# Stick-breaking heads without conditioning panels: nine panels move into layer one, and the scores are computed once and masked on VectorE

## The chip, the cores and the metric

One core of a Trainium2 chip runs the whole program. The metric is the device time of one execution in microseconds (us); less is better. TensorE is called PE in the rows, VectorE DVE, ScalarE ACT, GpSimd POOL, and SyncE, which issues the weight loads, SP.

## The reference

Input is x of 256 tokens by 1024 channels. A first block and two further layers follow each other. What matters here:

```python
# first block: u = rmsnorm(h); u_ssm, q, k, v = split(u @ w_in)
#   y_ssm  = s5_branch(u_ssm)                      32 groups, a linear recurrence over the tokens
#   y_attn = stick_breaking_attention(q, k, v)     8 heads of 64
#   h += (sigmoid gates * (y_ssm @ w_up_ssm, y_attn @ w_up_attn)) @ w_out;  h += relu(norm(h) @ w_ff1)^2 @ w_ff2
z = einsum("bqhd,bkhd->bhqk", q_blk, kf) * scale
mask = key_pos[None, :] < q_pos[:, None]
log_fail = where(mask, log_sigmoid(-z), 0.0)
after = cumsum(log_fail, axis=3, reverse=True) - log_fail
w = where(mask, exp(log_sigmoid(z) + after), 0.0)
# layers 0 and 1 (depth 2):
ada = c_act @ w_ada + b_ada        # (1, 3072) a layer; c_act = silu(c)
shift, scale, gate = split(ada, 3)
u = x * (1 + scale) + shift        # ... convolutions, latent attention of 8 heads, merge, w_o
```

## The kernel before

All activations lie in SBUF with channels on the partitions. The weights (about 177 MB) stream from HBM in **panels** of at most 1 MB, in the order that `schedule()` writes out by hand. Every engine walks this one list `ORDER` from front to back and does its own part of each step, so an engine that waits holds back all later steps of its own.

A panel lands in one of four slots of `raw` (`RAW = 4`, by its index in the list). ACT rounds it to `w_hi` (L842), DVE or POOL computes the rest `w_lo` (L1122, L744; POOL for gate panels 2 to 7 and the feed-forward), and PE does 48 matmuls of 256 columns, three for each product (L1617 to L1619). `w_hi` and `w_lo` have three slots (`HL = 3`); `next_splits` works ahead by at most three split panels, and from a split panel by fewer than four places of the list, from a conditioning panel by fewer than two.

Results go to two PSUM banks in turn, `pg[g % 2]`, where `g` counts the groups of all panels. `group_start(g)` makes PE wait until group `g - 2` has been read out (`take`, L848 on ACT, L1149 on DVE).

A **conditioning panel** (`ada_panel(i)`, 24 of them, 12 a layer) isn't split: PE reads it from `raw` (L1651) and gives its slot back itself. It takes a group like the others. `ada_take(i)` reads that bank on ACT into `root[:, 1, :]`, and `ada_turn(i)` (L1732, PE) turns it into two columns of a PSUM bank. `ada_end(part)` adds the bias on DVE.

The stick-breaking attention runs together with the recurrence of the first block, in eight **turns** m = 0 to 7 (and a last one, 8). In a turn:

- PE: `stick_fails(m)` (the scores a second time into `p_c`, then three products with `ntri` and `nones`), `ada_turn(m)`, `stick_scores(m+1)` into `p_z`, `bu(2m+1)` and `bu(2m+2)` (L1756), the gate panel m, `s5_out(m-1)` (L1773), `stick_out(m-1)`, and conditioning panel m+1. `bu(r)` waits for `state(r-2)`.
- DVE: `stick_weights(m-1)`, `stick_soft(m)`, `state(2m)` and `state(2m+1)`: eight instructions each on `p_bu` or `p_s` and the table `waves`. `state(r)` waits for `bu(r)` and, from r = 4, for `s5_out((r-4)/2)`.
- ACT: Exp of the weights, the rounding of a panel, Abs, Exp and Ln of the scores, and the sigmoids of the gate.
- POOL: the tables (L793 to L797) and `w_lo` of the gate panels. Before the turns it builds the block-diagonal inputs of the recurrence (`s5_diag`, L762 to L769).

Layer one (`l == 0`) begins with the latent panels (`q_lat`, `kv_lat`, `k_rope`), their norms (`latent_sums`, `latent_norm`, where `root[:, 1, :]` is ACT's square root of `kv_lat` and DVE inverts it, L1167), then panels `a2`, `a1`, `uq`, `ukv`, the long convolution on DVE (`conv_a`, L1517), eight heads of latent attention with a panel beside each, the branches and merges, `w_o` and the layer norm.

Of the kernel before, what the change touches and what calls it, by code (L numbers as in the profile page):

```python
# [19 lines left out]
P = 128  # L20
T = 256
# [56 lines left out]
ADA_PARTS = ((0, 14), (14, 17), (17, 20), (20, 24))  # L78
# [12 lines left out]
def schedule():  # L91
# [74 lines left out]
    ada_panel(0)  # L166
    step("ada_take", 0)
    for m in range(HEADS + 1):
# [8 lines left out]
        step("ada_turn", m)  # L177
# [34 lines left out]
    step("ada_turn", 9)  # L212
    ada_panel(10)
    step("ada_take", 10)
    panel("up_attn", 0, 1, "w_up_attn", 0, 512, WT, 512, 2)
    step("ada_turn", 10)
    half("glu", 0, "w_glu", W)
    ada_panel(11)
    step("glu_mul")
    step("split", "yg")  # L220
    step("ada_take", 11)
    step("ada_turn", 11)
    half("up_ssm", 0, "w_up_ssm", D)
    ada_panel(12)
    step("split", "u1")
    step("ada_take", 12)
    for n in range(4):
        panel("out", 0, n, "w_out", 0, 256 * n, KT, 256, 1)
        if n < 2:
            step("ada_turn", 12 + n)  # L230
        if n == 0:
            ada_panel(13)
            step("ada_take", 13)
        if n == 1:
            step("ada_end", 0)
        if n:
            norm_sums(1, n - 1)
    norm_steps(1, "u2", 14)
    chunks = DFF // W
    for c in range(chunks + 1):  # L240
        if c < chunks:
            for n in range(2):
                panel("ff1", 0, 2 * c + n, "w_ff1", 0, W * c + 256 * n, KT, 256, 1)
                if (c, n) == (0, 0):
                    step("ada_turn", 16)
                    step("ada_end", 1)
# [7 lines left out]
    norm_steps(2, ("u", 0), 17)  # L254

    for l in range(LAYERS):
        panel("q_lat", l, 0, "w_in_2", 0, CQ, KT, 256, 1)
        if l == 0:
            step("ada_turn", 19)
            step("ada_end", 2)  # L260
        else:
            step("ada_turn", 23)
            step("ada_end", 3)
# [25 lines left out]
        for h in range(HEADS + 2):  # L289
# [21 lines left out]
        for n in range(4):  # L311
            panel("merge1", l, n, "w_in_2", 0, CM + D + 256 * n, KT, 256, 1)
            if n == 1:
                step("ln_a_mean", l)
            if n == 3:
                step("ln_a_var", l)
        half("branch2", l, "w_c_out_2", D)
        for n in range(4):
            panel("merge2", l, n, "w_in_2", 0, CM + 2 * D + 256 * n, KT, 256, 1)
            if n == 0:  # L320
                step("ln_a_out", l)
            if n == 1:
# [4 lines left out]
        if l == 0:  # L327
            step("modulate_columns", 1)
        for n in range(4):
            panel("w_o", l, n, "w_o_2", 0, 256 * n, KT, 256, 1)  # L330
            if n:
                step("ln_mean", l, n - 1)
        if l == 0:
            ada_panel(20)
        step("ln_mean", l, 3)
        if l == 0:
            step("ada_take", 20)
        step("ln_centre", l)
        if l == 0:
            ada_panel(21)  # L340
            step("ada_turn", 20)
# [42 lines left out]
def build(nc, t, out, marks, dry):  # L384
# [3 lines left out]
    with ctx:  # L388
# [82 lines left out]
        mask1 = sb("mask1", [P, 384])  # L471
# [61 lines left out]
        stick_z = tmp[:, 4:7, :].rearrange("p a n -> p (a n)").rearrange("p (a n) -> p a n", a=2)  # L533
        stick = [stick_z[:, 0], stick_z[:, 1], stick_w[:, 0], stick_w[:, 1]]
# [151 lines left out]
        def _(pool):  # L686
# [12 lines left out]
            pool.memset(mask1[:, :], 1.0).then_inc(*c.step())  # L699
# [11 lines left out]
            for lo, w in ((0, 256), (256, 128)):  # L711
                pool.affine_select(out=mask1[:, lo:lo + w], in_=mask1[:, lo:lo + w], compare_op=ALU.is_gt,
                                          fill=0.0, base=0, pattern=[[1, w]], channel_multiplier=-1).then_inc(*c.step())
# [99 lines left out]
        def _(act):  # L813
# [199 lines left out]
            def stick_scores(hd, _):  # L1013

                act.wait_ge(sem("z"), over("z", hd))
                if hd == 0:
                    act.preload_act_table_set("natural_log_exp_and_others")
                else:

                    act.wait_ge(sem("soft"), over("soft", hd - 1))  # L1020
                fn(stick[0], p_z[:, 0:384], ACT.Abs).then_inc(*c.step())
                fn(stick[0], stick[0], ACT.Exp, scale=-1.0).then_inc(*c.step())
                fn(stick[0], stick[0], ACT.Ln, bias=1.0).then_inc(*c.event("log1p", hd))
# [83 lines left out]
        def _(dve):  # L1107
# [228 lines left out]

            def stick_soft(hd, _):

                dve.wait_ge(sem("log1p"), over("log1p", hd))
                stt(stick[1], p_z[:, 0:384], 0.0, stick[0], ALU.max, ALU.add).then_inc(*c.step())  # L1340
                tt(stick[1], stick[1], mask1[:, :], ALU.mult).then_inc(*c.event("soft", hd))

            def stick_weights(hd, _):
# [3 lines left out]
                stt(stick[2 + hd % 2], p_c[:, 0:384], 0.0, neg1[:, :], ALU.min, ALU.add).then_inc(*c.event("logw", hd))  # L1347

            def ada_end(part, _):
# [3 lines left out]
                for l in range(LAYERS):  # L1353
                    a, b = max(2 * first, 24 * l), min(2 * end, 24 * l + 24)
                    if a < b:
                        ps = p_z[:, 384 + a:384 + b] if part == 0 else p_c[:, a:b]
# [227 lines left out]
            def ln(l, _):  # L1584
                invert(("var", l))
                before = c.last
                for j in range(4):
# [7 lines left out]
                         stick_soft=stick_soft, stick_weights=stick_weights,  # L1595
# [9 lines left out]
        def _(pe):  # L1605
# [109 lines left out]
            def ada_turn(i, _):  # L1715
# [3 lines left out]
                ps = p_z[:, 384:512] if part == 0 else p_c  # L1719
                if part == 0:  # L1720
                    pe.wait_ge(sem("soft"), over("soft", min(i, HEADS - 1)))
                elif i == ADA_PARTS[1][0]:
                    pe.wait_ge(sem("logw"), over("logw", HEADS - 1))
                elif part > 1 and i == ADA_PARTS[part][0]:
                    pe.wait_ge(sem("ada"), over("ada", part - 1))
                    if part == 3:
                        pe.wait_ge(sem("probs_t"), over("probs_t", 0, HEADS - 1))
# [48 lines left out]
            def qk(dst, hd, stop):  # L1776

# [180 lines left out]
```

## Time and profile before

| | |
|---|---|
| median of 3 runs | 1209.64 us (1209.32 to 1210.97) |
| profiled execution | 1214.46 us, span 1212.6 us |
| busy share of the span | PE 88%, weight loads 82%, DVE 62%, ACT 45%, POOL 22% |
| mean granted TensorE clock | 0.929 |
| DMA queue of the weights | 177.22 MB, 46.0% of 16 engines |

The profiled execution is 4.8 us above the median; differences are taken within it. Times in timeline rows count from the start of its span.

### The profile page before, as it was taken

The numbers are of one execution on the slowest core, as the hardware profiler recorded it, in microseconds if no ns is written. First come the engines' busy times: TensorE is split into PE (matmuls) and PEld (weight loads), VectorE is DVE, ScalarE is ACT, GpSimd is POOL, SyncE is SP. The second block draws the span as 40 slices with busy tenths as digits, with TensorE's granted clock in tenths as the row PEclk, the third lists the DMA queues.
The fourth block names the chain that finished last, engine by engine and source line by source line (L and its number), as shares of the span: only waits on it lengthen the run. The fifth ranks groups of instructions, "written<-read, shape, count | busy, mean of one in ns | idle before, by whom it ended". The sixth has DMA issues, their size and how long they took to land.

```text
span 1212.6 us, 19568 instructions
## 1 busy us (share of the span) xinstructions
PE 1068.3 (88%) x8104; PEld 994.2 (82%) x8104; DVE 757.4 (62%) x1096; ACT 539.8 (45%) x620; POOL 262.9 (22%) x131
## 2 busy tenths in 40 slices
PE   4989999779799999969877998998789787989985
PEld 3968777579699999969876898998689776989984
DVE  4938887453624322267877797654657877886653
ACT  4543544432444434355422653542564234636432
POOL 3096771000586887401000000000010000000000
PEclk8978999889899999989988998998899898999997
DMA  7532434546564656365342444653637332544601
GB/s 246 192 119 81 155 113 140 183 129 209 184 199 140 208 177 202 123 208 159 105 139 74 136 139 139 199 184 105 193 106 223 97 107 77 177 147 133 210 29 35
DMA packets 159495, 179.56 MB, mean 148 GB/s; under 512 B 5040, under 2 KB 141744, under 8 KB 159408
## 3 DMA queue, kind: packets, MB, share of 16 engines
q1 hardware_dynamic: 159024, 177.22, 46.0%
q8 instruction: 64, 1.05, 0.4%
q0 software_dynamic: 384, 1.10, 0.3%
q14 instruction: 23, 0.19, 0.0%
HBM read 177.26 MB, written 1.05 MB: 147 GB/s over the span
## 4 chain that ended last, share of the span: by engine, by line
PE 56%; DVE 23%; issue 9%; ACT 8%; POOL 3%; DMA 1%; SPq 0%; DVEq 0%; ACTq 0%; POOLq 0%
PE pg L1617 16%; PE pg L1618 16%; PE pg L1619 16%; DVE area L1517 7%; ACT w_hi L842 4%; DVE area L1131 3%; DVE w_lo L1122 3%; ACT area L820 2%; DVE area L1139 2%; PE p_s L1611 1%; PE p_s L1707 1%; PE p_y L1773 1%; DVE area L1135 1%; DVE mx L1538 1%; DMA raw<-in_w_in 1%
## 5 line engine op out<-in xcount | busy, mean ns | idle before, releaser
L1617 PE MATMUL pg<-u_hi,w_hi 128*128 128x256 f32 x1664 | 492.6, 296 | 60.2 <-DVE u_lo L1131 38.3
L1618 PE MATMUL pg<-u_lo,w_hi 128*128 128x256 f32 x1664 | 482.3, 290 | 0.0
L1619 PE MATMUL pg<-u_hi,w_lo 128*128 128x256 f32 x1664 | 481.8, 290 | 0.0
L1617 PEld LDWEIGHTS pg<-u_hi,w_hi 128*128 128x128 f32 x1664 | 331.5, 199 | 70.1 <-issue 46.4
L1618 PEld LDWEIGHTS pg<-u_lo,w_hi 128*128 128x128 f32 x1664 | 331.7, 199 | 0.9
L1619 PEld LDWEIGHTS pg<-u_hi,w_lo 128*128 128x128 f32 x1664 | 330.7, 199 | 0.0
L1122 DVE TENSOR_TENSOR w_lo<-raw,w_hi 128x2048 fp32r<-128x2048 f32 (+3 forms) x115 | 247.3, 2158 | 127.6 <-ACT w_hi L842 127.4
L842 ACT ACTIVATE w_hi<-raw 128x2048 fp32r<-128x2048 f32 (+3 forms) x153 | 274.9, 1803 | 73.7 <-issue 38.6
L744 POOL TENSOR_TENSOR w_lo<-raw,w_hi 128x2048 fp32r<-128x2048 f32 x38 | 176.0, 4648 | 188.2 <-ACT w_hi L842 188.2
L848 ACT ACTIVATE area<-pg 128x512 f32<-128x512 f32 (+1 forms) x92 | 54.2, 589 | 170.2 <-PE pg L1619 158.3
L1517 DVE SCALAR_TENSOR_TENSOR area<-area,par 128x256 f32<-128x256 f32 x240 | 97.8, 480 | 0.8
L1617 PE MATMUL pg<-vb_hi,w_hi 128*128 128x256 f32 x320 | 91.7, 287 | 5.7 <-issue 3.8
L805 POOL COPY area<-area 64x2048 f32<-64x2048 f32 x2 | 8.0, 4014 | 400.9 <-DVE area L1131 400.9
L1618 PE MATMUL pg<-vb_lo,w_hi 128*128 128x256 f32 x320 | 91.3, 285 | 0.0
L1619 PE MATMUL pg<-vb_hi,w_lo 128*128 128x256 f32 x320 | 91.2, 285 | 0.0
L1617 PE MATMUL pg<-va_hi,w_hi 128*128 128x256 f32 x288 | 84.2, 292 | 3.7 <-DVE va_lo L1131 3.1
L1618 PE MATMUL pg<-va_lo,w_hi 128*128 128x256 f32 x288 | 82.9, 288 | 0.0
L1619 PE MATMUL pg<-va_hi,w_lo 128*128 128x256 f32 x288 | 82.9, 288 | 0.0
L1131 DVE TENSOR_TENSOR area<-area 128x512 f32<-128x512 f32 (+6 forms) x78 | 49.8, 638 | 34.2 <-ACT area L848 31.0
L1617 PEld LDWEIGHTS pg<-vb_hi,w_hi 128*128 128x128 f32 x320 | 62.0, 194 | 6.5 <-issue 4.9
L1149 DVE TENSOR_TENSOR h<-pg,h 128x512 f32<-128x512 f32 x36 | 24.9, 692 | 66.3 <-PE pg L1619 65.5
L820 ACT ACTIVATE area<-area 128x384 f32<-128x384 f32 (+6 forms) x67 | 37.1, 554 | 65.4 <-DVE area L1396 51.6
(200 smaller groups left out, 1327.3 us busy)
## 6 DMA issues: line engine op xcount, KB each, us to landing
raw<-in_w_in SPq DMA_DIRECT2D x68, 1024.0 KB, 5.3
raw<-in_w_ff SPq DMA_DIRECT2D x32, 1024.0 KB, 5.6
raw<-in_w_ada SPq DMA_DIRECT2D x24, 1024.0 KB, 5.1
raw<-in_w_gate SPq DMA_DIRECT2D x8, 1024.0 KB, 7.6
raw<-in_w_o SPq DMA_DIRECT2D x8, 1024.0 KB, 5.1
raw<-in_w_out SPq DMA_DIRECT2D x4, 1024.0 KB, 6.6
raw<-in_w_b_out SPq DMA_DIRECT2D x4, 1024.0 KB, 5.0
raw<-in_w_c_out SPq DMA_DIRECT2D x4, 1024.0 KB, 5.0
```

The costliest lines, as they stand in the source:

```text
L744: pool.tensor_tensor(w_lo[:, s, 0:n], raw[:, r, 0:n], w_hi[:, s, 0:n].bitcast(F32), ALU.subtract).then_inc(sem(f"raw_free{r}"), 1)
L820: return act.activation(out_, in_, func, **kw)
L842: act.activation(dst, src, ACT.Copy).then_inc(*(c.event("w_hi", q["s"]) if i == len(parts) - 1 else c.step()))
L848: act.activation(dst, src, func, **kw).then_inc(*c.bank_free(g))
L1122: ins = dve.tensor_tensor(dst, src, hi.bitcast(F32), ALU.subtract)
L1131: return dve.tensor_tensor(out_, a, b, op)
L1139: return dve.scalar_tensor_tensor(out=out_, in0=a, scalar=s, in1=b, op0=op0, op1=op1)
L1149: dve.tensor_tensor(out_, a, b, op).then_inc(*c.bank_free(g))
L1517: ins = dve.scalar_tensor_tensor(out=acc[:, j, :], in0=apad[:, j, k:k + T], scalar=w, in1=acc[:, j, :], op0=ALU.mult, op1=ALU.add)
L1617: pe.matmul(dst, w_h, x_h, start=first, stop=False)
L1618: pe.matmul(dst, w_h, x_l, start=False, stop=False)
L1619: return pe.matmul(dst, w_l, x_h, start=False, stop=last_)
```

## The change

- Panels 0 to 8 no longer stand in the turns. The 24 are renumbered: what were 9 to 19 are now 0 to 10, at the same places; 11 to 19 are in layer one; panel 20 moves ahead of `w_o`, 21 into its old place.
- The scores are computed once. DVE adds the mask to them (`stick_scores` on DVE, into two buffers `stick_z`); ACT and `stick_soft` read this copy, and the product with `mask1` is gone. ACT gets one more step a head (Relu before Exp).

```diff
-ADA_PARTS = ((0, 14), (14, 17), (17, 20), (20, 24))
+ADA_PARTS = ((0, 5), (5, 8), (8, 11), (11, 20), (20, 24))
+ADA_LATE = 11
@@ schedule(): the turns
     step("stick_scores", 0)
-    ada_panel(0)
-    step("ada_take", 0)
     for m in range(HEADS + 1):
...
             step("stick_fails", m)
-        step("ada_turn", m)
         if m + 1 < HEADS:
             step("stick_scores", m + 1)
...
             step("stick_out", m - 1)
-        if m < HEADS:
-            ada_panel(m + 1)
-            step("ada_take", m + 1)
     step("split", "ctx")
-    ada_panel(9)
-    step("ada_take", 9)
+    ada_panel(0)
+    step("ada_take", 0)
@@ layer one (l == 0)
         panel("k_rope", l, 0, "w_in_2", 0, CKR + ROPE - QK, KT, QK, 1)
+        if l == 0:
+            ada_panel(11)
         step("latent_sums", l)
...
         step("rope_k", l)
-        wide("a2", l, "w_in_2", A2, W)
+        if l == 0:
+            step("ada_take", 11)
+            ada_panel(12)
+        for n in range(2):
+            panel("a2", l, n, "w_in_2", 0, A2 + 256 * n, KT, 256, 1)
+            if (l, n) == (0, 0):
+                step("ada_turn", 11)
+                step("ada_take", 12)
...
         wide("a1", l, "w_in_2", A1, W)
+        if l == 0:
+            step("ada_turn", 12)
@@ heads h of layer one
             panel(job, l, n, "w_in_2", 0, at + 256 * n, KT, 256, 1)
+            if l == 0 and h in (1, 2, 3):
+                ada_panel(12 + h)
+                step("ada_take", 12 + h)
...
                 step("context", l, h - 2)
+            if l == 0 and h in (1, 2, 3):
+                step("ada_turn", 12 + h)
@@ merge1 to w_o: 16 and 17 around ln_a_mean, 18 and 19 around ln_a_var, 20 before w_o
             if n == 1:
+                if l == 0:
+                    ada_panel(16)
+                    step("ada_take", 16)
+                    ada_panel(17)
                 step("ln_a_mean", l)
+                if l == 0:
+                    step("ada_turn", 16)
+                    step("ada_take", 17)
             if n == 3:
+                if l == 0:
+                    step("ada_turn", 17)
+                    ada_panel(18)
+                    step("ada_take", 18)
                 step("ln_a_var", l)
+        if l == 0:
+            ada_panel(19)
+            step("ada_turn", 18)
+            step("ada_take", 19)
         half("branch2", l, "w_c_out_2", D)
...
             step("modulate_columns", 1)
+            ada_panel(20)
+            step("ada_take", 20)
@@ ACT
                 if i:
                     act.wait_ge(sem("ada_turned"), over("ada_turned", i - 1))
+                if i == ADA_LATE:
+                    act.wait_ge(sem("rstd"), over("rstd", ("lat_kv", 0)))
...
-                act.wait_ge(sem("z"), over("z", hd))
+                act.wait_ge(sem("masked"), over("masked", hd))
...
-                fn(stick[2 + hd % 2], stick[2 + hd % 2], ACT.Exp).then_inc(*c.event("w_stick", hd))
+                fn(stick_w[:, hd % 2], stick_w[:, hd % 2], ACT.Relu, scale=-1.0).then_inc(*c.step())
+                fn(stick_w[:, hd % 2], stick_w[:, hd % 2], ACT.Exp, scale=-1.0).then_inc(*c.event("w_stick", hd))
@@ DVE
+            def stick_scores(hd, _):
+                dve.wait_ge(sem("z"), over("z", hd))
+                tt(stick_z[hd % 2], p_z[:, 0:384], neg1[:, :], ALU.add).then_inc(*c.event("masked", hd))
...
-                stt(stick[1], p_z[:, 0:384], 0.0, stick[0], ALU.max, ALU.add).then_inc(*c.step())
-                tt(stick[1], stick[1], mask1[:, :], ALU.mult).then_inc(*c.event("soft", hd))
+                stt(stick_s, stick_z[hd % 2], 0.0, stick_s, ALU.max, ALU.add).then_inc(*c.event("soft", hd))
...
-                stt(stick[2 + hd % 2], p_c[:, 0:384], 0.0, neg1[:, :], ALU.min, ALU.add).then_inc(*c.event("logw", hd))
+                tt(stick_w[:, hd % 2], p_c[:, 0:384], stick_z[hd % 2], ALU.add).then_inc(*c.event("logw", hd))
@@ PE, stick_fails
-                qk(p_c, hd, False)
-                pe.matmul(p_c[:, 0:T], ntri[:, :], stick[1][:, 0:T], start=False, stop=False)
+                pe.matmul(p_c[:, 0:T], ntri[:, :], stick_s[:, 0:T], start=True, stop=False)
...
-                qk_rest(p_c, hd, False)
```

The mask `mask1` and its four instructions on POOL at the start are gone. `ada_turn` writes to `p_z` below panel 11 and to `p_y` from there; its waits follow the new places.

## Rows read from the trace of the kernel before

**Rows 1.** Windows of two turns: sum, PE, PEld, DVE, ACT, POOL, clock, DMA
```profile
165.30:179.81 14.51, 14.51 (x112) 11.24 (x111) 12.93 (x22) 8.99 (x13) 10.17 (x6) 1.00 0.45 145
179.81:195.81 16.00, 16.00 (x112) 12.73 (x111) 12.15 (x20) 7.76 (x10) 4.56 (x1) 0.89 0.41 133
```

**Rows 2.** Timeline of PE in turn 3
```profile
129.55 0.62 PE L1773 MATMUL p_y<-area 128*32 128x256 f32 x4
...
132.20 1.07 PE L1651 MATMUL pg<-raw,silu_c 128*32 128x256 f32 x16
133.20 0.70 PE L1779 MATMUL p_c<-area 64*128 64x256 f32 x2
...
135.41 0.50 PE L1732 MATMUL p_z<-pick,root 128*128 128x1 f32 x4
...
137.10 0.45 PE L1756 MATMUL p_bu<-area 32*128 32x256 f32 x1
...
144.06 0.63 PE L1773 MATMUL p_y<-area 128*32 128x256 f32 x4
```

**Rows 3.** Timeline of DVE: mask product, state(6), and the start of state(8)
```profile
129.99 1.48 DVE L1131 TENSOR_TENSOR area<-area,mask 128x384 f32<-128x384 f32 x1
131.69 0.69 DVE L1131 TENSOR_TENSOR area<-p_bu,waves 128x512 f32<-128x512 f32 x1 [0.22 <-PE p_y L1773]
...
135.54 1.42 DVE L1131 TENSOR_TENSOR area<-p_bu,waves 128x512 f32<-128x512 f32 x2
...
149.28 0.69 DVE L1131 TENSOR_TENSOR area<-p_bu,waves 128x512 f32<-128x512 f32 x1
```

**Rows 4.** Waits of DVE in turns 1 to 7: total, times, longest
```profile
DVE area L1131 <- PE p_y L1773: 7.3, 5, 3.1
```

**Rows 5.** Timeline of POOL and DVE where they hold each other up
```profile
61.85 2.69 POOL L764 TENSOR_TENSOR rows<-area 128x256 f32<-128x256 f32 x1
...
68.88 0.62 POOL L764 TENSOR_TENSOR rows<-area 128x256 f32<-128x256 f32 x1
...
142.03 4.57 POOL L744 TENSOR_TENSOR w_lo<-raw,w_hi 128x2048 fp32r<-128x2048 f32 x1
...
143.23 3.51 DVE L1135 TENSOR_SCALAR area<-area 128x256 f32<-128x256 f32 x1
```

**Rows 6.** Timeline of all engines, end of the turns
```profile
202.54 1.92 ACT L842 ACTIVATE w_hi<-raw 128x2048 fp32r<-128x2048 f32 x1 [2.81 <-DMA raw<-in_w_up_attn]
...
204.49 2.29 DVE L1122 TENSOR_TENSOR w_lo<-raw,w_hi 128x2048 fp32r<-128x2048 f32 x1 [3.40 <-ACT w_hi L842]
...
211.88 0.69 DVE L1131 TENSOR_TENSOR rows<-p_s,waves 128x512 f32<-128x512 f32 x1
...
214.52 0.77 PE L1732 MATMUL p_z<-pick,root 128*128 128x1 f32 x3 [3.49 <-ACT root L848]
...
224.85 0.55 PE L1617 MATMUL pg<-va_hi,w_hi 128*128 128x256 f32 x1 [3.14 <-DVE va_lo L1131]
```

**Rows 7.** Timeline in layer one: first a2 matmul, inverse of the kv_lat root
```profile
549.62 0.38 PE L1617 MATMUL pg<-u_hi,w_hi 128*128 128x256 f32 x1
...
552.99 1.75 DVE L1167 RECIPROCAL rows<-root 128x256 f32<-128x256 f32 x1
```

**Rows 8.** Timeline: DVE before the convolution, PE after it
```profile
584.02 2.29 DVE L1122 TENSOR_TENSOR w_lo<-raw,w_hi 128x2048 fp32r<-128x2048 f32 x1 [2.03 <-ACT w_hi L842]
...
611.38 0.55 PE L1617 MATMUL pg<-u_hi,w_hi 128*128 128x256 f32 x1 [8.60 <-DVE area L1149]
```

**Rows 9.** Timeline of PE: layer-norm sums of the merges, start of w_o
```profile
729.40 3.68 PE L1611 MATMUL p_s<-area,ones 128*128 128x256 f32 x8 [3.09 <-DVE area L1517]
...
746.47 3.68 PE L1611 MATMUL p_s<-area,ones 128*128 128x256 f32 x8 [1.89 <-ACT area L820]
...
822.34 0.55 PE L1617 MATMUL pg<-u_hi,w_hi 128*128 128x256 f32 x1 [3.07 <-DVE u_lo L1131]
```

**Rows 10.** Timeline: DVE's low half of the panel in head 3 of layer one
```profile
648.81 2.29 DVE L1122 TENSOR_TENSOR w_lo<-raw,w_hi 128x2048 fp32r<-128x2048 f32 x1 [2.01 <-ACT w_hi L842]
```

More of the change, by code:

```diff
@@ L211, in schedule @@
     panel("up_attn", 0, 0, "w_up_attn", 0, 0, WT, 512, 2)
-    step("ada_turn", 9)
-    ada_panel(10)
-    step("ada_take", 10)
+    step("ada_turn", 0)
+    ada_panel(1)
+    step("ada_take", 1)
     panel("up_attn", 0, 1, "w_up_attn", 0, 512, WT, 512, 2)
-    step("ada_turn", 10)
+    step("ada_turn", 1)
     half("glu", 0, "w_glu", W)
-    ada_panel(11)
+    ada_panel(2)
     step("glu_mul")
     step("split", "yg")
-    step("ada_take", 11)
-    step("ada_turn", 11)
+    step("ada_take", 2)
+    step("ada_turn", 2)
     half("up_ssm", 0, "w_up_ssm", D)
-    ada_panel(12)
+    ada_panel(3)
     step("split", "u1")
-    step("ada_take", 12)
+    step("ada_take", 3)
     for n in range(4):
@@ L229, in schedule @@
         if n < 2:
-            step("ada_turn", 12 + n)
+            step("ada_turn", 3 + n)
         if n == 0:
-            ada_panel(13)
-            step("ada_take", 13)
+            ada_panel(4)
+            step("ada_take", 4)
         if n == 1:
@@ L244, in schedule @@
                 if (c, n) == (0, 0):
-                    step("ada_turn", 16)
+                    step("ada_turn", 7)
                     step("ada_end", 1)
@@ L258, in schedule @@
         if l == 0:
-            step("ada_turn", 19)
+            step("ada_turn", 10)
             step("ada_end", 2)
@@ L321, in schedule @@
                 step("ln_a_out", l)
+                if l == 0:
+                    step("ada_turn", 19)
+                    step("ada_end", 3)
             if n == 1:
@@ L332, in schedule @@
                 step("ln_mean", l, n - 1)
+            elif l == 0:
+                step("ada_turn", 20)
         if l == 0:
-            ada_panel(20)
+            ada_panel(21)
         step("ln_mean", l, 3)
-        if l == 0:
-            step("ada_take", 20)
         step("ln_centre", l)
         if l == 0:
-            ada_panel(21)
-            step("ada_turn", 20)
             step("ada_take", 21)
@@ L1018, in stick_scores @@
                 else:
[L1020 to L1023, printed above, removed]
+                    act.wait_ge(sem("fails"), over("fails", hd - 1))
+                fn(stick_s, stick_z[hd % 2], ACT.Abs).then_inc(*c.step())
+                fn(stick_s, stick_s, ACT.Exp, scale=-1.0).then_inc(*c.step())
+                fn(stick_s, stick_s, ACT.Ln, bias=1.0).then_inc(*c.event("log1p", hd))
             def stick_weights(hd, _):
@@ L1355, in ada_end @@
                     if a < b:
-                        ps = p_z[:, 384 + a:384 + b] if part == 0 else p_c[:, a:b]
+                        ps = (p_y if first >= ADA_LATE else p_z)[:, 384 + a:384 + b]
                         tt(ada[:, l, a - 24 * l:b - 24 * l], ps, col(("b_ada", l), a - 24 * l, b - a),
@@ L1718, in ada_turn @@
                 part = next(k for k, (a, b) in enumerate(ADA_PARTS) if i < b)
[L1719 to L1722, printed above, removed]
+                ps = (p_y if i >= ADA_LATE else p_z)[:, 384:512]
+                if i == 0:
                     pe.wait_ge(sem("logw"), over("logw", HEADS - 1))
-                elif part > 1 and i == ADA_PARTS[part][0]:
+                elif i == ADA_LATE:
+                    pe.wait_ge(sem("k_roped"), over("k_roped", 0))
+                elif i == ADA_PARTS[part][0]:
                     pe.wait_ge(sem("ada"), over("ada", part - 1))
-                    if part == 3:
-                        pe.wait_ge(sem("probs_t"), over("probs_t", 0, HEADS - 1))
                 for s, v in emptied([q["g"]]):
@@ L1774, in s5_out @@
                 ins.then_inc(*event("cx", j))
-            def qk(dst, hd, stop):
-                rows, f = slice(64 * (hd % 2), 64 * (hd % 2) + 64), hd // 2
-                pe.matmul(dst[:, 0:T], k1[rows, f, 0:P], q1[rows, f, :], start=True, stop=stop)
-            def qk_rest(dst, hd, stop):
-                rows, f = slice(64 * (hd % 2), 64 * (hd % 2) + 64), hd // 2
-                return pe.matmul(dst[:, T:T + P], k1[rows, f, P:T], q1[rows, f, P:T], start=True, stop=stop)
             def stick_scores(hd, _):
@@ L1789, in stick_scores @@
                 if hd:
-                    pe.wait_ge(sem("soft"), over("soft", hd - 1))
-                qk(p_z, hd, True)
-                qk_rest(p_z, hd, True).then_inc(*event("z", hd))
+                    pe.wait_ge(sem("masked"), over("masked", hd - 1))
+                rows, f = slice(64 * (hd % 2), 64 * (hd % 2) + 64), hd // 2
+                pe.matmul(p_z[:, 0:T], k1[rows, f, 0:P], q1[rows, f, :], start=True, stop=True)
+                pe.matmul(p_z[:, T:T + P], k1[rows, f, P:T], q1[rows, f, P:T], start=True, stop=True).then_inc(*event("z", hd))
             def stick_fails(hd, _):
```

28 lines of the change are left out of this document (13 added, 15 removed).

## The prediction

> **What bounds the kernel now.** The page's first table comes first: TensorE is busy for 88% of the span, which suggests that work taken off it counts. The windows by turn qualify that. One turn, 165.30 to 179.81, lasts 14.51 us with PE recorded busy all through at a full clock; the next lasts 16.00 at 0.89 [rows 1]. Full records don't say what sets a period, so I followed an earlier turn's chain through the timeline. DVE starts `state(6)` at 131.69 and ends its eight instructions at 136.96, 5.27 us [rows 3]. PE begins `bu(8)` 0.14 later, at 137.10, and `s5_out` behind the gate panel's 48 matmuls at 144.06, 6.96 after that [rows 2]. From the `s5_out` before, at 129.55 [rows 2], to `state(6)`, which waited for it, were 2.14. 5.27 + 0.14 + 6.96 + 2.14 = 14.51: this loop over two engines gives the period of the full-clock turn [rows 1]. The waits confirm it: in turns 1 to 7 DVE stands still five times for `p_y`, written by `s5_out`, 7.3 us in all [rows 4]. Neither a conditioning panel nor the second scores lie in the loop; they lie on PE while DVE does `state`. Behind the turns PE waits openly [rows 6], as it does in layer one at the convolution and in the merges [rows 8, 9].
>
> **Removed in the turns.** A turn on PE loses one conditioning panel (133.20 - 132.20 = 1.00), its turn (0.50), and the second scores (about 0.62 + 0.42 of what stands at `p_c` and behind it; the first row of them is 0.70) [rows 2]: about 2.45 us, 19.6 over eight turns. By the loop above this is worth nothing: `stick_fails` and `bu` come earlier, and PE then waits for `state` ahead of `bu`. DVE loses a mask product, 0.56 to 1.48 us (1.48 in turn 3 [rows 3]), and gets an add of the same 384 columns: even. ACT's Relu adds some 0.5 us a head, as its other steps on these columns take, and lies beside DVE's `state`; without that cover it would be 0.5 a head, 4 in all. POOL's four mask instructions lay before the tables, hidden behind the first panels: nothing.
>
> The low clock: the turn at 0.89 was 16.00 - 14.51 = 1.5 longer than the one at 1.00 [rows 1], and one more of the middle turns was like it. With PE idle some 2.4 us in every turn I expect lower clocks in more of them, and choose two more turns at half that price (a part of the loop is DVE's): +1.5. Bounds: 0, and six turns at 1.5, +9. Against it, POOL and DVE hold each other up less. DVE's 128x256 step takes 3.51 us beside POOL's 4.57 us `w_lo` [rows 5] where half of a 512-column step's 0.69 [rows 3] is due; that turn lasts 149.28 - 131.69 = 17.59 [rows 3], 3.1 above 14.51. Without a panel ahead of it POOL's `w_lo` of the next gate starts about 2.4 us earlier and misses that step; a turn on, it can meet the start of `s5_y` instead, of which I estimate 1.9 (4.57 less the 2.4 and a start 0.3 in). I take -3.1 + 1.9 = -1.2, bounds -3.1 and +3.1. In the Trainium skill, "SBUF — State Buffer", section "Who interferes with whom", a VectorE instruction with two SBUF inputs and a GpSimd instruction contend for one port pair, and the one that issued first keeps it to its end; this trace agrees (3.51 and 2.69 against 0.62), and by that rule `stick_soft`, which now has two SBUF inputs, can be held as well, for up to what a POOL row lasts, 4.57; the sum above has one hold in the turns, and with a second of the same 1.9 it would be 1213.1.
>
> The start: without panels 0 and 1 the low half of gate panel 1 moves ahead of the tables, where one POOL step may be held as at 61.85, 2.69 - 0.62 = 2.1 later [rows 5]; but DVE then doesn't have that low half (2.59 there, 2.29 elsewhere [rows 8]) inside turn 0. 2.1 - 2.4 = -0.3. **Start and turns: 1.5 - 1.2 - 0.3 = 0**, bounds -3.4 and +12 by the pieces; since the clock and the hold each came in only some of the turns before, I let the range reach +6.
>
> **Removed at the end of the turns.** This part is on the path. The rounding of `up_attn` waits 2.81 for its load, since a conditioning panel holds the slot; DVE waits 3.40 for the rounding and spends 2.29 on the low half, all ahead of `state(15)` [rows 6]. After the change the panel lands a turn earlier, and both pass into a turn where DVE waits for PE anyway: -(3.40 + 2.29) = -5.7. If DVE's order puts the low half back in the same place, only the wait goes, -3.4. Then PE: `state(15)` ends at 212.57 (211.88 + 0.69), `up_attn` starts at 224.85, 12.28 later [rows 6]. In it `ada_turn(8)` waits 3.49 for ACT and `s5_out` behind it runs at half clock. Without these, `s5_out`, the gelu chain on DVE and the split of `va` remain. Taking 3.49 and 0.2 of half clock off, 8.6 remain: -3.7. Bounds: -2 (DVE's chain sets more of it than PE) and -5. **Together -9.4**, bounds -5.4 and -11.
>
> **Added in layer one.**
> Panel 11 (1.00 on PE, as in [rows 2]) stands before `latent_sums`, where PE waits for DVE's squares: nothing, and its own length without that wait. The larger cost is a PSUM bank. `a2`'s first group uses the bank that panel 11 filled. `ada_take(11)` overwrites the root that DVE inverts from 552.99 for 1.75, to 554.74 [rows 7], so it waits for that end. The take then needs about 0.5 us (a 512-column step on DVE takes 0.69 [rows 3]; estimate): PE can start `a2` at about 555.3 (the take begun as the inversion ends) instead of 549.62 [rows 7], **+5.7**. Behind a stand of nearly 5 us PE comes back at a lower clock, as at 214.52 (0.77 for three of its matmuls, 0.50 for four in turn 3 [rows 6, 2]); a first stretch of some 3 us at about half speed is +1.5, an estimate. `a2`'s second panel waits for `ada_take(12)`, which stands behind `a2`'s first take on ACT: +0.8; two turns at 0.44, +0.9. Panel 12 lies within the stand, nothing. Sum at `uq`: **+8.9**, bounds +6 (nothing but the bank) and +10.
>
> Is this absorbed later? Behind it, DVE's low half at 584.02 waits 2.03 for ACT, which waits for PE's `uq`; the convolution starts after it, and PE's 8.60 wait at 611.38 is for DVE [rows 8]. So DVE is delayed as PE is, and the 8.60 stays. I carry the +8.9 in full.
>
> In the heads of layer one DVE sets the pace; panels 13, 14, 15 and their turns lie in PE's waits, nothing (without them 3 x 1.5 = 4.5). The later `w_lo` wait, 2.01 in head 3 [rows 10], goes once, because a conditioning panel ahead lets `w_hi` be taken earlier: -1.6, bounds 0 and -2. In the merges, 16 and 17 stand before sums that wait 3.09 (two panels are 2.1: hidden); turn 16 is +0.44; take 18 and panel 18 stand before sums that wait 1.89 [rows 9], turn 17 and the take's place on ACT delay them by about 1.75; panel 19 +1.07 (at the clock it would meet there), turns 18 and 19 +0.44 each: 0.44 + 1.75 + 1.07 + 0.88 = +4.1. After the filled 3.09 wait PE is warmer, -0.8: **+3.3**, bounds +1.5 and +5. Panel 20 lies in the 3.07 wait ahead of `w_o` [rows 9], its turn +0.44; panels 20 and 21 went from places behind `w_o` where PE waited for DVE, no gain. **Sum of layer one: 8.9 - 1.6 + 3.3 + 0.4 = +11.0**, bounds +8 and +14.
>
> **The sum.** 0 - 9.4 + 11.0 = +1.6. The profiled execution took 1214.46, 1212.6 of it span, so this gives 1216.1. It stood 0.4% above the median of the runs; on 1209.64 the same difference gives **1211.2**.
>
> **The rivals.** (a) Faster, one mechanism: the bank wait at `a2` is absorbed by PE's 8.60 wait at 611.38 [rows 8]. It decides if DVE reaches the convolution by work that doesn't hang on `uq`. Then 1211.2 - 8.6 = 1202.6. For it: the wait is that long; against it: the 2.03 wait of DVE ahead of the convolution is for ACT. 0.15. (b) The heads are bound by PE, as 14.51 busy of 14.51 says [rows 1], and the 19.6 us come off: about 1191.6. Against it: the waits for `p_y` [rows 4]. 0.05. (c) The POOL holds vanish and no new one comes, and the lower clock adds nothing: -3 to -5, 1207; 0.08. (d) Slower: PE idles in each turn and its clock falls in each: three more at the whole 1.5 than I took, and a hold as before: 4.5 + 1.2 = +5.7, 1216.9; 0.20. The Trainium skill, "TensorE: Matmul & The Clock Gate", section "HAM oscillation — how this bites in real kernels", describes this: waits that return in each round of a loop let the clock fall in each round; the trace has both, the row at 0.89 and the one at 1.00 [rows 1]. (e) Slower: the panels in the merges aren't covered (takes wait in ACT's order, nine panels and turns at 1.5 = 13.5 instead of about 9.5): +4, 1215; 0.15.
>
> **How the numbers follow.** The forecast, gains at the end of the turns about equal to the bank wait and the merges, has 0.37. Within 0.2% (2.4 us, about what a measurement of this kernel can tell) is 1207.2 to 1212.1. Faster, a + b + c: 0.28; same 0.37; slower, d + e: 0.35. The range leaves out b and the ends of d: 1204.5 to 1218; (a)'s 1202.6 lies just below it, so that about 2 in 10 is outside. The forecast's own range is 1207 to 1214.
>
> **What would show it.** Right: a full-clock turn still lasts about 14.5, with PE waiting for `state` before L1756; DVE's waits for `p_y` stay; `up_attn` starts near 215; PE waits 5 to 6 us for ACT ahead of `a2`'s first matmul; the wait after the convolution is still about 8.6. Wrong: turns near 12 (b); that wait near zero (a); most turns at 15 or 16 (d); waits ahead of the sums of the merges longer than before (e).

## The result

| | median us | runs | against before, 95% interval |
|---|---|---|---|
| before | 1210.06 | 4 | |
| changed | 1221.27 | 4 | 1.0094 (1.0075 to 1.0114) |

The change costs 0.94%, about 11 us, where +1.6 was forecast and the range ended at 1218. The two profiled spans are 1212.6 and 1219.5, 6.9 apart. The profiled execution of before (1214.46) stood 4.4 above the median of the table, that of the changed kernel (1221.24) on its median; the places of the loss are read from the two traces, and the remaining 4 us between 6.9 and 11.2 can't be placed by them.

The windows of the changed kernel, from one `bu(2m+2)` to the next (from the left: start and end, sum, busy times, granted clock, DMA share, GB/s), answer to [rows 1]:

```profile
106.15:122.14 15.99, 14.14 (x86) 11.49 (x87) 13.19 (x20) 9.18 (x11) 10.42 (x3) 0.88 0.44 131
122.14:139.56 17.42, 15.56 (x87) 12.47 (x87) 11.88 (x20) 8.31 (x11) 16.18 (x14) 0.79 0.20 62
139.56:156.82 17.26, 15.40 (x87) 12.30 (x87) 12.92 (x23) 8.77 (x12) 6.02 (x2) 0.80 0.19 62
156.82:174.00 17.18, 15.32 (x87) 12.23 (x87) 14.96 (x21) 8.31 (x11) 16.32 (x13) 0.80 0.20 62
174.00:191.13 17.13, 15.27 (x87) 12.18 (x87) 13.04 (x23) 8.77 (x12) 4.90 (x2) 0.80 0.18 61
```

Four turns in a row last 17.1 to 17.4 at a granted clock of 0.79 to 0.80, and in each PE stands still for 1.86 (sum less PE's busy time). No turn of before looked like this: its five turns between the same marks lasted 16.02, 14.52, 17.59, 16.03 and 14.50, at clocks of 0.89, 1.00, 1.00, 0.89 and 1.00. The timeline of PE in one turn shows where it stands:

```profile
136.57 1.13 PE L1787 MATMUL p_s<-area 32*128 32x256 f32 x4
139.56 2.04 PE L1787 MATMUL p_bu<-area 32*128 32x256 f32 x4 [1.85 <-DVE area L1161]
141.52 0.58 PE L1650 MATMUL pg<-u_hi,w_hi 128*128 128x256 f32 x1
...
149.27 0.41 PE L1804 MATMUL p_y<-area 128*32 128x256 f32 x2
```

and DVE in the same turn:

```profile
134.15 0.69 DVE L1161 TENSOR_TENSOR area<-p_bu,waves 128x512 f32<-128x512 f32 x1 [4.59 <-PE p_y L1804]
...
137.99 1.42 DVE L1161 TENSOR_TENSOR area<-p_bu,waves 128x512 f32<-128x512 f32 x2
139.51 0.56 DVE L1161 TENSOR_TENSOR area<-p_z,neg 128x384 f32<-128x384 f32 x1
...
151.41 0.69 DVE L1161 TENSOR_TENSOR area<-p_bu,waves 128x512 f32<-128x512 f32 x1 [3.13 <-PE p_y L1804]
```

The loop of the prediction is all there: `state` 134.15 to 139.41 (5.26), then 0.15 to `bu`, then 149.27 - 139.56 = 9.71 to `s5_out`, then 2.14: 17.26. Three of the four links are what they were [rows 2, 3]; the one on PE grew from 6.96 to 9.71. Four products of `bu` take 2.04 there, those of `p_s` just ahead of the pause 1.13: instructions of the same shape, before and after a stand of 1.85. The chain that ended last goes through the same three places, turn after turn:

```profile
139.56 2.04 PE p_bu L1787 x4
141.59 0.51 PE pg L1650
...
149.34 1.88 PE p_y L1804 x16
151.41 0.70 DVE area L1161
...
156.82 2.04 PE p_bu L1787 x4
```

The waits in the stretch 106.15 to 207 confirm it. The second row answers to [rows 4] (7.3, 5 times):

```profile
PE p_bu L1787 <- DVE area L1161: 10.5, 6, 1.9
...
DVE area L1161 <- PE p_y L1804: 15.3, 6, 4.6
```

**The way out of the turns.** `state(15)` ends at 213.40 + 0.69 = 214.09, `up_attn` begins at 223.11:

```profile
213.40 0.69 DVE L1161 TENSOR_TENSOR rows<-p_s,waves 128x512 f32<-128x512 f32 x1
...
223.11 0.36 PE L1650 MATMUL pg<-va_hi,w_hi 128*128 128x256 f32 x1 [3.40 <-DVE va_lo L1161]
```

At the sigmoid of gate panel 6 the changed kernel is 7.0 behind (200.80 against 193.79); at the end of `state(15)` it is 1.5 behind [rows 6], at `up_attn` 1.7 ahead, and from there it drifts to 0.5 ahead in the feed-forward.

**Layer one.** ACT and PE at `a2` (timelines), which answer to [rows 7], then the wait behind the convolution, which answers to [rows 8]:

```profile
554.30 0.38 ACT L875 ACTIVATE root<-pg 128x256 f32<-128x256 f32 x1 [3.03 <-DVE rows L1197]
```
```profile
546.17 2.42 PE L1644 MATMUL p_s<-area,ones 128*128 128x256 f32 x10 [1.01 <-ACT area L847]
...
554.83 0.55 PE L1650 MATMUL pg<-u_hi,w_hi 128*128 128x256 f32 x1 [4.66 <-ACT root L875]
...
563.79 0.36 PE L1650 MATMUL pg<-u_hi,w_hi 128*128 128x256 f32 x1 [0.94 <-ACT root L875]
...
620.20 0.55 PE L1650 MATMUL pg<-u_hi,w_hi 128*128 128x256 f32 x1 [8.60 <-DVE area L1179]
...
736.41 1.99 PE L1644 MATMUL p_s<-area,ones 128*128 128x256 f32 x8 [1.18 <-DVE area L1550]
...
754.22 1.99 PE L1644 MATMUL p_s<-area,ones 128*128 128x256 f32 x8 [1.70 <-ACT area L847]
```

PE waits 4.66 for the take of panel 11 and 0.94 for that of panel 12, and the 8.60 behind the convolution is untouched, to the hundredth. Ahead of the sums of the merges 1.18 and 1.70 are left of 3.09 and 1.89 [rows 9], and the first sums take 1.99 where they took 3.68.

### The profile page after: what moved, and what is told of

It reads as the page before. It is cut to its first block, busy times and chain, and to the rows that moved or that the text cites. A ratio compares the mean times of both kernels' runs of the same rounds, so it can differ in the third digit from the quotient of the medians.

```text
span 1219.5 us, 19506 instructions
## 1 busy us (share of the span) xinstructions
PE 1065.0 (87%) x8072; PEld 992.8 (81%) x8072; DVE 757.0 (62%) x1097; ACT 544.0 (45%) x628; POOL 261.9 (21%) x128
## 4 chain that ended last, share of the span: by engine, by line
PE 53%; DVE 26%; issue 9%; ACT 8%; POOL 3%; DMA 1%; DVEq 0%; SPq 0%; ACTq 0%; POOLq 0%
PE pg L1650 17%; PE pg L1651 16%; PE pg L1652 16%; DVE area L1550 7%; DVE area L1161 4%; ACT w_hi L869 3%; DVE w_lo L1152 3%; ACT area L847 2%; DVE area L1169 2%; DVE rows L1197 1%; PE p_s L1740 1%; DVE p_bu L1161 1%; DVE area L1179 1%; DVE p_bu L1346 1%; PE p_bu L1787 1%
## 5 line engine op out<-in xcount | busy, mean ns | idle before, releaser
L847 ACT ACTIVATE area<-area 128x384 f32<-128x384 f32 (+6 forms) x79 | 43.4, 549 | 60.8 <-DVE area L1429 51.6
```

The lines of the kernel that those rows point to most:

```text
L847: return act.activation(out_, in_, func, **kw)
```

## The experiments

Two theories of the turns stood against each other. **A:** PE's work was useful as cover; with 2.45 us of it gone PE stands still before every `bu(2m+2)`, and the clock that it gets after the stand is lower, so the PE link of the loop grows. **B:** the order on DVE and ACT did it (the mask add between two states, the longer chain of the scores), whatever PE does. For layer one: **A** says that the bank wait at `a2` is the cost, **C** that a later wait would take its place.

The table gives, from each trace, the mean of five turns between six starts of `bu(2m+2)` (from about 106), the granted clock of that stretch, and the waits of PE for DVE ahead of `bu` that lie in it (so not the one that ends at its start).

| kernel | median us | against before | turn | clock | PE waits at `bu` |
|---|---|---|---|---|---|
| before | | | 15.73 | 0.96 | 0.9, once |
| scores_only | 1216.77 | 1.0044 (1.0027 to 1.0062) | 16.51 | 0.90 | 4.2, 5 times |
| panels_only | 1215.83 | 1.0028 (1.0015 to 1.0041) | 15.99 | 0.89 | 3.1, 5 times |
| changed | 1221.27 | 1.0094 (1.0075 to 1.0114) | 17.00 | 0.81 | 9.3, 5 times |
| fill4 | 1209.94 | 0.9990 (0.9975 to 1.0004) | 16.05 | 0.91 | 0.7, once |
| fill8 | 1211.26 | 1.0010 (0.9993 to 1.0026) | 15.16 | 1.00 | none |
| fill_late | 1227.36 | 1.0146 (1.0133 to 1.0160) | 18.17 | 0.89 | 9.3, 5 times |
| a2_free | 1215.58 | 1.0032 (1.0020 to 1.0043) | 16.44 | 0.85 | 9.3, 5 times |
| own_row | 1223.19 | 1.0114 (1.0101 to 1.0127) | 16.86 | 0.81 | 9.3, 5 times |
| tail7 | 1207.74 | 0.9986 (0.9966 to 1.0005) | 16.90 | 0.90 | 0.9, once |
| tail7_once | 1209.48 | 0.9989 (0.9967 to 1.0011) | 16.98 | 0.90 | 6.9, 5 times |
| fill4_a2 | 1203.70 | 0.9957 (0.9935 to 0.9979) | 16.05 | 0.91 | 0.7, once |
| fill6_a2 | 1203.44 | 0.9956 (0.9938 to 0.9974) | 14.85 | 1.00 | none |
| own_row_fill6 | 1207.37 | 0.9982 (0.9967 to 0.9997) | 14.85 | 1.00 | none |

The runs were made in three series, each on another chip, and the kernel before had medians of 1211.35 (30 runs; the first four experiments), 1209.40 (35; tail7, tail7_once, fill8, fill4_a2) and 1210.07 (18; the rest). The changed kernel was measured only together with the 1210.06 of the result. Between series the ratios are the safer comparison; where they and the medians give different sizes, both stand below. One run of before among the 35 took 2650.72; a median doesn't feel it.

A trace is one execution. Those of before, panels_only, tail7 and tail7_once lie 2 to 4.5 above the median of their kernel, that of fill4_a2 (1210.86) is its slowest of 12, that of fill6_a2 (1199.76) its fastest of 7. The changed kernel, own_row and a2_free are alike up to the end of the turns, and their five turns still average 17.00, 16.86 and 16.44: a difference of some tenths between two traces shows nothing.

### scores_only and panels_only: each half of the change alone

scores_only takes of the diff the parts on `stick_scores`, `stick_soft`, `stick_weights`, `stick_fails` and the masks; panels_only takes all the rest.

> The kernel before with the scores computed once and masked on DVE; all conditioning panels stay in the turns. Theory A (a PE pause before bu(2m+2) lowers the granted clock of the gate panel behind it, 7.8 us instead of 6.0): the pause here is only about the 1.0 us of the removed second scores, so I expect turns between 14.5 and 17.2 us and a total of 1210 to 1217. Theory B (the new DVE add between the two states, and ACT's longer order, make the turn longer, whatever PE does): turns of about 17.2 as in the changed kernel, total 1219 to 1224, since nothing is gained at the end of the turns.

> The kernel before with the nine panels moved; the scores stay computed twice with the mask product. Theory A: the pause before bu(2m+2) is about 0.9 us instead of 1.85, turns between 14.5 and 17.2; gain at the way out about 8 us, cost in layer one about 8 us, total 1210 to 1221. Theory B: turns as before, total about 1210.

Each half costs, by 0.44% and 0.28%, and the sum, 0.72%, is under the whole, 0.94%, by no more than the intervals allow. Both totals are within theory A's spans. In scores_only the turns are longer, with a wait of PE at each `bu(2m+2)`. Those of panels_only are hardly longer than before's (15.99 for 15.73), but before's include the one of 17.59, which POOL lengthened by 3.1; what fell there is the clock, 0.89 for 0.96, although DVE and ACT do what they did before, which B doesn't explain. Its turns lose only 0.7 against before up to gate panel 6, and most of its 0.28% comes from `a2` (9 us from `kv_lat` to `uq`) against the gain at the way out. The windows of panels_only show turns of three lengths side by side:

```profile
122.05:139.54 17.49, 16.87 (x90) 13.20 (x91) 12.55 (x20) 6.85 (x9) 16.19 (x14) 0.81 0.19 61
139.54:154.06 14.52, 13.90 (x90) 10.68 (x91) 12.94 (x23) 9.13 (x13) 6.06 (x2) 1.00 0.20 73
154.06:170.05 15.99, 15.37 (x91) 12.15 (x91) 14.49 (x21) 6.86 (x9) 15.13 (x13) 0.88 0.20 67
```

With the same 0.62 us pause in each, the turn takes 14.52 at a clock of 1.00, 15.99 at 0.88 and 17.49 at 0.81. So the price of 1.5 that the prediction used is that of a turn in which the clock was low for a part; a turn in which it is low for about twice as long costs 3.0. The trace of panels_only also holds the gain at the way out: it is 7.0 ahead of before at the first take of `glu`.

### fill4, fill8 and fill_late: useless work in the pause, more of it, and the same work elsewhere

```diff
@@ PE, stick_fails, of the changed kernel; n = 4 or 8
+                for _ in range(n):
+                    pe.matmul(p_c[:, 0:T], ntri[:, :], stick_s[:, 0:T], start=True, stop=True)
                 pe.matmul(p_c[:, 0:T], ntri[:, :], stick_s[:, 0:T], start=True, stop=False)
@@ fill_late instead: PE, ahead of the 48 matmuls of a gate panel
+                    if job == "gate":
+                        group_start(g)
+                        for _ in range(8):
+                            pe.matmul(pg[g % 2][:, 0:P], ntri[:, :], ones[:, :], start=True, stop=True)
```

The useless products are overwritten by the next one with `start=True`.

> The changed kernel with four useless products (ntri by the fail terms into p_c, overwritten at once) ahead of the three of stick_fails in every turn, about 2 us of PE work at full clock. Theory A: the pause before bu(2m+2) is filled, the clock stays up, turns go from 17.2 to 14.5 to 15, total 1221.3 less 5 to 6 turns at 2.3 to 2.7, about 1207. Theory B: PE's added work is hidden or adds to the turn, total 1221 to 1225.

> The changed kernel with eight useless products in every turn, about 4 us. Theory A: about 1.9 us fill the pause, the other 2.1 us lie on the loop at full clock: turns of about 16.6, total near 1210 + 7 x 2.1 less what the last low turns cost, about 1220 to 1225, at a granted clock near 1.00 in the turns. If PE work alone (and no pause) sets the turn, each useless product costs the same from the first: 1221 + 16.

> The changed kernel with eight useless 128-column products, about 1.8 us of PE work, at the start of each gate panel, behind bu(2m+2) instead of ahead of stick_fails. The pause before bu(2m+2) stays. Theory A (the pause counts, not the amount of PE work): the clock falls in every turn as before, and the work is added: turns of 17.2 + 1.8 or more, total 1221.3 + 8 x 1.8 = 1236 or more. If the amount of work in a turn counts and not the pause: turns at full clock, 14.5 + 1.8 = 16.3, total about 1215 to 1218.

Adding work took 11 us off: 1221.27 to 1209.94 (12.6 by the ratios). DVE and ACT do the same steps in the same order in both, so B, by which that order costs the time whatever PE does, is out. The total lies 3 above A's 1207, and the clock still fell in three of the five turns. The timelines of PE have the whole filler in one row, first fill4, then fill8:

```profile
147.81 1.99 PE L1823 MATMUL p_c<-area,ntri 128*128 128x256 f32 x8
```
```profile
145.90 3.72 PE L1823 MATMUL p_c<-area,ntri 128*128 128x256 f32 x16
```

The next products start 1.83 and 3.55 behind the filler's start, so a useless product is 0.44 to 0.46. In fill8 the turn is filled by PE, at a full clock in all five:

```profile
121.23:136.26 15.03, 15.03 (x105) 12.43 (x104) 12.06 (x19) 8.32 (x11) 14.25 (x12) 1.00 0.22 71
136.26:151.28 15.02, 15.02 (x104) 12.42 (x103) 12.93 (x22) 8.77 (x12) 8.03 (x4) 1.00 0.18 70
```

This gives the number that the prediction should have begun with. PE's own work in a turn of the changed kernel, at full clock, is 15.03 - 3.55 = 11.5 us; before it was 11.5 + 2.45 = 13.9, in a loop of 14.5. Call the difference the room, an estimate: 0.6 before, 3.0 in the changed kernel, 2.0 in panels_only (14.5 - 11.5 - 1.0), 1.2 in fill4, 0.3 with six products (below). 1.1 to 1.4 us of it isn't seen as a stand: where `bu(2m+2)` must wait, its products run alone behind those of `bu(2m+1)` (1.10 behind 1.12 in fill4), while in fill8 the two interleave and take 1.13 together. In fill4 the clock still falls in some turns (14.51 at 1.00, but also 16.00 at 0.89 and 17.52 at 0.81); in the two traces with a room of 0.3 it falls in none. My expectation for fill8, turns of 16.6 and 1220 to 1225, was wrong for that reason: I had taken the 1.85 seen at the low clock for all the slack that there is.

In fill_late the pause of 1.86 stays in all five turns, and so do lower clocks (0.98, 0.84, 0.90, 0.83, 0.90):

```profile
122.77:142.05 19.28, 17.43 (x102) 14.32 (x103) 11.87 (x20) 8.31 (x11) 16.17 (x14) 0.84 0.18 55
142.05:159.95 17.90, 16.04 (x102) 13.11 (x103) 12.93 (x23) 8.76 (x12) 6.01 (x2) 0.90 0.17 59
```

The total, 1227.4, lies between the two expectations: the turns grow by 1.17, less than the 1.8 of the added work, since the clock falls less than in the changed kernel: 18.17 is 1.9 above the 16.3 of a full clock, where 17.00 is 2.5 above 14.5. So neither expectation was right as it stood: the amount of work counts for something, but doesn't do away with the low clock. About as much work as in fill4, put behind the pause, costs 6 us; put into it, it gains 11.

### a2_free and own_row: the bank wait in layer one

a2_free puts panels 11 and 12 beside the heads; own_row leaves them at `a2`, and takes panel 11 early into `odd_z`, so that nothing waits for the inversion:

```diff
@@ a2_free: panels 11 to 15 beside heads 1 to 5
-            if l == 0 and h in (1, 2, 3):
-                ada_panel(12 + h)
+            if l == 0 and h in (1, 2, 3, 4, 5):
+                ada_panel(10 + h)
@@ own_row
             ada_panel(11)
+            step("ada_take", 11)
         step("latent_sums", l)
...
-                if i == ADA_LATE:
+                if i == ADA_LATE + 1:
                     act.wait_ge(sem("rstd"), over("rstd", ("lat_kv", 0)))
-                take(g, root[:, 1, :], pg[g % 2][:, 0:256])
+                take(g, odd_z[:, 0:256] if i == ADA_LATE else root[:, 1, :], pg[g % 2][:, 0:256])
```

> The changed kernel with panels 11 and 12 taken away from a2: panels 11 to 15 stand beside heads 1 to 5 of layer one. Theory A (PE waited 5 to 6 us at a2 for the bank of panel 11, and again behind it): all but 0 to 1.5 us of the +8.8 that stands at uq goes, total about 1213. Rival C (PE would wait for the latent norm's chain later anyway, at uq): total 1219 to 1221.

> The changed kernel with one edit in layer one: the take of panel 11 goes to a row buffer of its own and stands ahead of latent_sums, so it waits for no inversion on DVE and frees the bank before a2. Theory A: the first a2 take comes 5 to 7 us earlier against its neighbours than in the changed kernel; total about 1221.3 - 6 = 1215. Rival C (the wait passes to panel 12's take or to uq): not below 1218.

a2_free is at 1215.6, 5.7 under the changed kernel (7.5 by the ratios), 2.6 above A's 1213. From `kv_lat` to `uq` it is level with before (0.0, where the changed kernel lost 9.3), and gives 3.7 back in the heads, where the two panels now stand. 2.0 of the 5.6 between the two spans is there before layer one begins, where the kernels are alike; the edit gives the rest. The clock of the stretch 550 to 560 is 0.66 in the changed kernel and 1.00 in a2_free (windows of each):

```profile
550.00:560.00 10.00, 5.34 (x33) 5.20 (x30) 9.51 (x12) 5.65 (x5) 3.23 (x1) 0.66 0.50 164
```
```profile
550.00:560.00 10.00, 10.00 (x86) 10.00 (x85) 9.62 (x9) 5.74 (x6) 4.01 (x1) 1.00 0.18 53
```

own_row did not gain: 1223.2 (1.0114 against 1.0094, intervals that overlap). Its wait for the take is gone, and against before the first take of `a2` comes 3.7 earlier than in the changed kernel (5 to 7 expected), but other rows of PE show what came instead:

```profile
546.59 3.64 PE L1644 MATMUL p_s<-area,ones 128*128 128x256 f32 x10 [2.09 <-ACT area L847]
...
558.40 0.61 PE L1764 MATMUL p_y<-pick,odd_z 128*128 128x1 f32 x4 [0.23 <-DVE area L1161]
560.72 0.39 PE L1650 MATMUL pg<-u_hi,w_hi 128*128 128x256 f32 x1 [1.72 <-DVE w_lo L1152]
```

The take stands ahead of the squares on ACT, the sums start later and take 3.64 instead of 2.42, DVE's chain of the latent norm ends later (the last step of the rotation starts at 557.92 instead of 556.29), and behind it DVE's low half of `a2`'s second panel is late by 1.72. From `kv_lat` to `uq` own_row loses 8.5 where the changed kernel lost 9.3. Rival C was right: freeing the bank in this way passes the wait on. Of what was tried, only moving both panels away removed the cost; an early take that doesn't stand ahead of the squares was not tried.

### tail7 and tail7_once: seven panels back in the turns

```diff
@@ turns; the other two panels stand beside heads 1 and 2 of layer one
+        if m < 7:
+            step("ada_turn", m)
...
+        if m + 1 < 7:
+            ada_panel(m + 1)
+            step("ada_take", m + 1)
```

> The kernel before with seven of the nine panels left in the turns; only the last two are moved, to heads 1 and 2 of layer one, and scores stay computed twice. Theory A: the turns stay full of PE work (14.5 to 16 us, as before), the 8 us at the way out of the turns are gained, and the heads of layer one take two panels for 0 to 2 us: about 1204 (1202 to 1207). Rival D (the gain at the way out needs the turns free of all panels): 1209 to 1212.

> As the kernel with seven panels in the turns, with the scores computed once and masked on DVE. Theory A: the pause before bu(2m+2) grows by the 1.0 us of the removed scores, the clock falls in about every second turn, 3 to 6 us more than with double scores: 1207 to 1210. Theory B (only DVE's and ACT's order counts): as much slower again as the changed kernel's turns, 10 or more.

tail7 computes the scores twice, as before, tail7_once once. tail7 was meant to keep the cover and take the gain at the way out; it came to 1207.7 with an interval that holds 1. Its trace has two steps of DVE held for 3.5 us by POOL's `w_lo` where before had one (timeline of DVE):

```profile
145.49 3.56 DVE L1146 TENSOR_SCALAR area<-area 128x256 f32<-128x256 f32 x1
...
180.31 3.54 DVE L1146 TENSOR_SCALAR area<-area 128x256 f32<-128x256 f32 x1
```

That is about 3.1 of the 5.8 that its five turns take longer than before's; the rest is the clock, 0.90 for 0.96, and at gate panel 6 it is 6.6 behind, nearly as far as the changed kernel. From there to the first take of `up_attn` it gains 8.3, as forecast. Whether every execution has the second held step was not tried. tail7_once is at 1209.5, within its expectation; its trace has three held steps (3.6, 3.6 and 4.1) and the same 0.90, so theory A's "3 to 6 us more" than tail7 isn't shown, and for a difference between the two their intervals are too wide.

The room orders the kernels only roughly. tail7 does before's PE work in these turns (room 0.6), and the first of its five falls to 0.81 with no stand of PE on record in it; a2_free has the changed kernel's turns (room 3.0), and the first of its five is at a full clock. Windows of tail7, then of a2_free:

```profile
107.32:124.84 17.52, 17.52 (x108) 13.90 (x110) 11.72 (x19) 7.01 (x10) 4.05 (x1) 0.81 0.31 102
```
```profile
106.82:121.34 14.52, 12.66 (x86) 10.01 (x87) 13.22 (x20) 9.49 (x11) 10.44 (x3) 1.00 0.46 144
121.34:137.34 16.00, 14.14 (x87) 11.49 (x87) 11.93 (x20) 8.33 (x11) 15.14 (x13) 0.87 0.20 67
```

What decides in which turn the clock falls stays open.

### fill4_a2, fill6_a2, own_row_fill6: both repairs at once

> The changed kernel with four useless products in every turn and panels 11 to 15 beside heads 1 to 5 instead of at a2. If the two costs are independent: 1209.9 less 5.7 = about 1204. If they share a cause: 1208 to 1210.

> Six useless products (2.7 us) in every turn and panels 11 to 15 beside heads 1 to 5: turns of 14.5 to 15, at a clock of 1.00, and no turn of 19 (a DVE step held by POOL) if the shifted order misses it as with eight: 1201 to 1204.

> Six useless products in every turn, and the take of panel 11 in a row buffer of its own ahead of latent_sums. If the two are independent: about 1210 - 6 = 1204, and 1201 if the two panels there cost less than beside heads 4 and 5 (3.7 us).

The two costs add by the medians: 1209.94 - 5.7 = 1204.2 was expected, 1203.70 measured. By the ratios 0.9928 would be due and 0.9957 (0.9935 to 0.9979) was measured, a shortfall of 3.5 us that the intervals of the four kernels leave open. fill6_a2 is at 1203.4, 0.44% under before, and can't be told from fill4_a2. Its turns (windows):

```profile
105.83:120.36 14.53, 14.53 (x100) 11.97 (x99) 13.22 (x20) 8.32 (x11) 10.45 (x3) 1.00 0.47 145
120.36:134.86 14.50, 14.50 (x100) 11.97 (x100) 11.81 (x20) 8.32 (x11) 13.76 (x11) 1.00 0.22 73
134.86:149.43 14.57, 14.57 (x101) 12.04 (x100) 13.22 (x23) 8.77 (x12) 8.62 (x4) 1.00 0.22 73
149.43:165.56 16.13, 15.18 (x103) 12.32 (x101) 14.94 (x21) 8.32 (x11) 15.35 (x12) 1.00 0.21 66
165.56:180.07 14.51, 14.51 (x98) 11.96 (x98) 13.03 (x23) 8.77 (x12) 5.93 (x3) 1.00 0.22 73
```

Four of five have the period of the loop, 14.5. The other, 16.13 at a full clock, holds a step of DVE that POOL delays (2.55 at 150.05). own_row_fill6 has the same turns, in a trace close to its median (1206.96), and is 3.9 slower: from `kv_lat` to `uq` it loses 7.1 where fill6_a2 loses nothing, and in the heads it gets 3.6 of that back. Its expected 1204 failed with own_row's.

## Why the prediction was wrong, step by step

**What bounds the turns: right.** The loop over DVE and PE stands in the changed kernel with the same 5.3, 0.15 and 2.14; four of five turns of fill6_a2 last 14.50 to 14.57. That PE's removed work gains nothing in the turns was right too.

**The low clock in the turns: the step that failed.** The prediction named the mechanism, with PE idle some 2.4 us in every turn, and then chose "two more turns at half that price", +1.5, with +9 as the bound. Measured: four turns in a row at 17.1 to 17.4, 2.6 to 2.9 above the loop's 14.5, and 7.0 lost by gate panel 6. Two choices were wrong. The count: the removed 2.45 made the room in a turn 0.6 + 2.45 = 3.0, and with it no turn after the first came back above 0.80 (a2_free, with the same turns: 1.00, 0.87, then 0.80); in panels_only, with a room of 2.0, two of five did reach 0.99 or 1.00. The price: 1.5 is the price of a turn at 0.89; at 0.80 it is 2.75. I halved it on the ground that "a part of the loop is DVE's", though 1.5 was already a difference of whole turns. Rival (d) was this, priced at +5.7 over the forecast; that it was given 0.20 and the range cut at 1218 made the miss. The rule of the Trainium skill that the prediction named ("TensorE: Matmul & The Clock Gate", "HAM oscillation — how this bites in real kernels") fits the changed kernel's trace: a wait that returns in each round, a clock of 0.80 in four rounds running. That fill6_a2 undoes it with idle work agrees with it. The rule doesn't cover all that the traces show: the clock also fell to 0.89 in before and to 0.81 in tail7 in turns without any stand of PE on record.

**POOL and DVE: right that the 3.51 step goes, wrong on the new one.** The hold a turn later (2.56 at 157.44, 2.1 above a free step) isn't new: the same step took 2.14 at 154.65 before. So -3.1 + 0.4 was due for the prediction's -3.1 + 1.9. `stick_soft` was held as well, as the prediction allowed: 2.03 at 112.83, where a step of 384 columns alone takes 0.56. In the changed kernel these holds don't show: its turns with and without one last as long, as DVE waits for `p_y` anyway.

**The way out: right, a little large.** `state(15)` regained 5.5 (5.7 forecast), from its end to `up_attn` 12.28 became 9.02 (-3.3, -3.7 forecast). Behind `up_attn` 1.2 went again, for which I had no term.

**Layer one, to `uq`: right in size, 9.3 for 8.9**, and in mechanism as far as the changed kernel's own waits go (4.66 and 0.94 for ACT's takes, clock 0.66). What own_row adds is that these waits cover another one of nearly the same length; I had written of the bank as "the larger cost". Its 8.60 was not absorbed: rival (a) is out, 8.60 before and after.

**The heads: right.** -1.8 where -1.6 was forecast.

**The merges and `w_o`: mis-sized.** +3.7 forecast, +0.3 measured (7.0 behind at the end of the heads, 7.3 at the start of layer two). The sums behind the panels ran in 1.99 instead of 3.68, twice: 3.4 back, where the prediction allowed 0.8. Rival (e) is out.

**The sum.** +7.0 - 8.7 (5.5 and 3.3, with rounding) + 1.2 + 7.8, and 0.4 less in layer two, is the +6.9 of the spans; forecast were 0 - 9.4 + 11.0. The errors, +7 in the turns and -3 in layer one, leave half of the distance to +11.2. The other half is the distance of the profiled before to its own median, which no experiment placed. The forecast's way from 1216.1 to 1211.2 carried the same distance, so the miss in the medians is 10 us and in the spans 5.3.

## What to carry to other kernels

Before removing work from TensorE, write down how much of each round of the loop it would stand still at full clock; the removed work adds to that, and in a round at the lower clock all that it still has on the path is stretched. Price such a turn by the lowest clock that any row shows, and for all rounds, as a case of its own rather than as an average. A panel that one wants elsewhere needs a place where the engine, its bank and the takes behind it are all free: check the next wait behind the one that is removed.

## What the runs showed of the hardware

Useless work gave time back: with 1.8 us of idle matmuls a turn (four products) the changed kernel went from 0.94% above the original to level with it (0.9990), and with panels 11 and 12 off `a2` as well to 0.43% below. In a loop of 14.5 us, the two kernels with a room of 0.3 us a turn (worked out as above) kept a granted clock of 1.00 in all of ten turns; over five turns it was 0.96 in before and 0.90 in tail7 with a room of 0.6, 0.91 with 1.2 (fill4), 0.90 with 1.5 (scores_only and tail7_once: 14.5 - 11.5 - 1.5), 0.89 with 2.0 (panels_only), and 0.81, 0.81 and 0.85 with 3.0 (changed, own_row, a2_free). With one and the same pause of 0.62, turns of 1.00, 0.88 and 0.81 follow each other (panels_only), so neither the pause nor the work in a turn fixes its clock; at what moments the clock is granted anew was not tried.
